# Hybrid decoder step on one core: unscaled token rows for the experts, the last cached values in front of weight slabs, stacked dilation-16 cache rows, and two state-space heads in two row strips

## The reference

```python
# state-space model: the decay between two positions, per head
rel = jnp.where(causal, cum[:, :, None] - cum[:, None, :], -jnp.inf)
w = cb[..., None] * jnp.exp(rel) * dtc[:, None]

# sample attention, group g: keys at distances 0, dil, ..., 128*dil (those that exist)
keys = jnp.concatenate([buf[:, :, 0], k], axis=1)
vals = jnp.concatenate([buf[:, :, 1], v], axis=1)
idx = wb + jnp.arange(S)[:, None] - dil * jnp.arange(129)[None, :]
p = softmax(q . keys[idx]);  o = p @ vals[idx]

# experts: the rows are normalised per token, h = x * rsqrt(mean(x*x) + eps) * gain
out = out + combine[..., e:e + 1] * swiglu(h, w_up[e], w_down[e])
```

## Time and profile before

| | |
|---|---|
| time of one execution, median of 3 (lowest, highest) | 2194.18 us (2193.89, 2195.5) |
| the profiled execution: its time, its span | 2194.97 us, 2193.2 us |
| mean granted TensorE clock of the profiled execution | 0.995 |
| layer 0 mixer and dense channel mixer | from 0 to some 840 us |
| layer 1 mixer and routing | to 1310.5 us |
| experts | 1310.5 to 2183 us |

### The profile page before, as it was taken

One profiled execution on the slowest core, in us unless ns is written; L12 is line 12 of the kernel. 1 busy time (PEld: TensorE's weight loads), 2 busy tenths in 40 slices (PEclk: granted clock), 3 DMA queues, 4 the chain that ended last, 5 costly groups with the idle time before them and its releaser, 6 DMA issues.

```text
span 2193.2 us, 43454 instructions
## 1 busy us (share of the span) xinstructions
PE 2155.8 (98%) x19497; PEld 1338.5 (61%) x19497; DVE 603.4 (28%) x1179; ACT 373.4 (17%) x671; POOL 103.9 (5%) x153
## 2 busy tenths in 40 slices
PE   7999999999999999999999989999999999999998
PEld 6777777767777777777777763534343434343435
DVE  5395323433110124933244331010101010101013
ACT  3323424311000023243333020000000000000000
POOL 2001020000000000011200010000000000000001
PEclk9999999999999999999999989999999999999999
DMA  5434535684444453354465759999999999999996
GB/s 160 135 101 138 165 109 158 174 242 135 135 137 114 132 168 123 116 160 126 131 176 141 245 228 378 410 405 415 406 415 406 414 407 415 402 412 404 407 415 247
DMA packets 298137, 548.66 MB, mean 250 GB/s; under 512 B 12153, under 2 KB 228603, under 8 KB 281504
## 3 DMA queue, kind: packets, MB, share of 16 engines
q1 hardware_dynamic: 289964, 535.84, 68.1%
q10 hardware_dynamic: 6644, 5.58, 0.8%
q0 software_dynamic: 1344, 4.45, 0.5%
HBM read 527.15 MB, written 22.50 MB: 251 GB/s over the span
## 4 chain that ended last, share of the span: by engine, by line
PE 95%; DVE 3%; issue 1%; ACT 1%; ACTq 0%; DMA 0%; DVEq 0%
PE bank L980 93%; PE bank L986 2%; ACT mem L1839 1%; DVE mem L2589 0%; DVE col L2592 0%; DVE mem L2560 0%; DVE mem L2281 0%; DVE mem L2602 0%; DVE mem L2605 0%; ACTq L2148 0%; DMA hv<-in_ssm_d_dram 0%; DVE mem L2285 0%; ACT L1839 0%; DVE mem L2600 0%; ACTq L2151 0%
## 5 line engine op out<-in xcount | busy, mean ns | idle before, releaser
L980 PE MATMUL bank<-mem 128*32 128x256 f32 (+11 forms) x11936 | 1007.3, 404 | 15.8 <-issue 5.3
L980 PEld LDWEIGHTS bank<-mem 128*32 128x32 f32 (+4 forms) x11936 | 567.8, 121 | 436.9 <-issue 236.0
L980 PE MATMUL bank<-hflat,mem 128*128 128x288 f32 (+1 forms) x2944 | 717.3, 407 | 1.3 <-ACT hflat L1839 0.7
L980 PEld LDWEIGHTS bank<-hflat,mem 128*128 128x128 f32 (+1 forms) x2944 | 538.0, 188 | 164.3 <-issue 20.3
L1839 ACT ACTIVATE mem<-bank 128x288 f32<-128x288 f32 (+7 forms) x344 | 157.2, 462 | 814.4 <-PE bank L980 775.4
L980 PE MATMUL bank<-mem,steps 128*32 128x384 f32 (+1 forms) x3072 | 289.8, 539 | 0.0
L980 PEld LDWEIGHTS bank<-mem,steps 128*32 128x32 f32 x3072 | 95.3, 110 | 191.1 <-issue 190.3
L2285 DVE SCALAR_TENSOR_TENSOR hflat<-hflat,bank 128x512 f32<-128x512 f32 x24 | 15.1, 682 | 411.1 <-ACT hflat L1839 411.1
L1839 ACT ACTIVATE hflat<-bank 128x512 f32<-128x512 f32 (+1 forms) x40 | 19.6, 554 | 566.0 <-PE bank L980 566.0
L2285 DVE SCALAR_TENSOR_TENSOR mem<-mem,bank 128x288 f32<-128x288 f32 (+1 forms) x93 | 43.2, 478 | 216.7 <-ACT mem L1839 178.6
L1839 ACT ACTIVATE mem<-mem 128x1152 f32<-128x1152 f32 (+8 forms) x102 | 80.2, 786 | 99.9 <-DVE mem L2359 71.4
(11 more groups left out here) (239 smaller groups left out, 720.3 us busy)
## 6 DMA issues: line engine op xcount, KB each, us to landing
mem<-in_w_moe_up_dram SPq DMA_DIRECT2D x64, 2048.0 KB, 18.1
mem<-in_w_moe_down_dram SPq DMA_DIRECT2D x56, 2048.0 KB, 18.9
mem<-in_w_moe_up_dram SPq DMA_DIRECT2D x32, 2304.0 KB, 20.1
mem<-in_w_in_dram SPq DMA_DIRECT2D x70, 1024.0 KB, 5.5
mem<-in_w_moe_up_dram SPq DMA_DIRECT2D x16, 1536.0 KB, 19.3
mem<-in_w_ffn_up_dram SPq DMA_DIRECT2D x44, 512.0 KB, 4.6
mem<-in_cache_kv_w_dram SPq DMA_DIRECT2D x26, 512.0 KB, 5.9
mem<-in_w_ffn_down_dram SPq DMA_DIRECT2D x16, 704.0 KB, 5.5
```

The source lines that it names most:

```text
L980: return mm(out, lhsT, rhs, start=start, stop=stop, skip_group_check=True)
```

## The change

Four edits, each with its bookkeeping.

1. **Token rows.** Both halves of `htok` are copied unscaled. The picking matrix of the first round holds each token's factor (`pick_scale`) in place of 1. After the gather, ScalarE multiplies `htok` by the factors in place, and only then may GpSimd scatter the rows. After a round VectorE sets `pick_scale` to 1.
2. **Last cached values.** The two slabs that stood in front of the wait for `att_o` and of the values of sequence 7 are issued behind them.
3. **Dilation-16 rows.** Two residues are stacked in 128 partitions: a 128 by 2 by 256 block (`kb_far`) by two DMAs. Keys: four transposes of 128 by 128 in place of eight of 64 by 128. Turned weights: two matmuls for four. Values: four matmuls of 128 rows by 128 columns for four of 64 rows by 256 columns. ScalarE's copy of the turned weights is 128 by 256 for 64 by 512.
4. **State-space heads.** ScalarE copies the running sums once more to partitions 32 to 39 (`cum_below`), and the odd head of a pair takes its row from there, so the two matmuls of a pair lie in different row strips of the array.

```diff
-        pT2 = view(arena, 9216 + 5 * P, 4, P)
+        pT2 = view(arena, 9216 + 5 * P, 2, P)
+        cum_below = steps[32:32 + SH, 2 * T:3 * T]
-        kb_half = [v[0:64, 5:9, :] for v in whole] + [view(steps[0:64, :], 0, 4, 256), view(over[0:64, :], 1280, 4, 256)]
+        kb_far = [v[:, 5:7, :] for v in whole] + [view(steps, 0, 2, 256), view(over, 1280, 2, 256)]
...
-                sp.dma_start(kb_half[i], c2048[:, 0:4, which, :]).then_inc(k_in[i], 16)
+                for e in range(2):
+                    sp.dma_start(kb_far[i][64 * e:64 * e + 64], c2048[:, e:4:2, which, :]).then_inc(k_in[i], 16)
...
                 for b in range(4, 7):
                     load_cache(L, 1, b)
-                weights_until(out0 + RING + 3)
                 sp.wait_ge(*filled(("att_o", L, 1)))
                 load_cache(L, 1, 7)
                 weights_until(out0 + RING + 4)
...
-            pool.wait_ge(token_rstd, 1)
-            pool.wait_ge(tok_half0, 3)
-            for b, (t0, n) in enumerate(BLK):
-                half = htokv[0:n, b, :, 0:P]
-                gp.tensor_tensor(half, half, t_rstd[0:n, b:b + 1].unsqueeze(2).to_broadcast([n, 4, P]), ALU.mult
-                                 ).then_inc(tok_scaled, 1)
-            pool.wait_ge(tok_scaled, 3)
-            pool.wait_ge(tok_half1, 3)
...
                 pool.wait_ge(slots_ready, r + 1)
+                pool.wait_ge(tok_scaled, 3 * r + 3)
...
-                close_bank(put(acc[:, 0:T], row_to(h, P), dts[0:SH, 2, :]), ("wdecay", L, h))
+                if h % 2 == 0:
+                    ins = put(acc[:, 0:T], row_to(h, P), dts[0:SH, 2, :])
+                else:
+                    row = ident[32:32 + SH, 32 + h:33 + h].to_broadcast([SH, P])
+                    ins = put(acc[:, 0:T], row, cum_below)
+                close_bank(ins, ("wdecay", L, h))
...
-                    for i in range(8):
-                        ins = turn(acc[:, 64 * i:64 * i + 64], half[:, i // 2, P * (i % 2):P * (i % 2) + P])
+                    for i in range(4):
+                        ins = turn(acc[:, P * i:P * i + P], far[:, i // 2, P * (i % 2):P * (i % 2) + P])
...
-                for r in range(4):
-                    c = 640 + 64 * r
-                    ins = turned(acc[0:64, P * r:P * r + P], kv_rows[:, c:c + 64])
+                for a in range(2):
+                    ins = turned(acc[:, P * a:P * a + P], kv_rows[:, 640 + P * a:768 + P * a])
...
                 for q in range(4):
-                    ins = put(acc[32 * q:32 * q + 32, c0:c0 + 256], pT2[0:64, q, cols], half[:, q, :],
+                    a, h0_ = q // 2, P * (q % 2)
+                    ins = put(acc[32 * q:32 * q + 32, c0 + h0_:c0 + h0_ + P], pT2[:, a, cols], far[:, a, h0_:h0_ + P],
                               False, b % 2 == 1)
...
-                pe.wait_ge(tok_scaled, 3)
+                pe.wait_ge(tok_half0, 3)
                 pe.wait_ge(tok_half1, 3)
...
                 act.wait_ge(*at("dt_cum", L))
+                step(fn(cum_below, dts[0:SH, 2, :], ACT.Copy))
...
-                copy_out(pT2[0:64].rearrange("p a r -> p (a r)"), key, psum(key)[0:64, :])
+                copy_out(pT2.rearrange("p a r -> p (a r)"), key, psum(key)[:, 0:2 * P])
...
-                    if half:
-                        ins = fn(out, src, ACT.Copy, scale=t_rstd[0:n, b:b + 1])
...
+                    ins = fn(out, src, ACT.Copy)
...
+            token_copies(1)
             act.wait_ge(token_rstd, 1)
-            token_copies(1)
...
+                for b, (t0, n) in enumerate(BLK):
+                    fn(htok[0:n, b, :], htok[0:n, b, :], ACT.Copy, scale=pick_scale[0:n, b:b + 1]).then_inc(tok_scaled, 1)
+                act.wait_ge(tok_scaled, 3 * r + 3)
+                act.sem_inc(wait_passed, 1)
                 act.wait_ge(x_scattered, 96 * (r + 1))
                 load_rows(1)
...
             dve.wait_ge(top_apart, 1)
+            step(ve.tensor_copy(pick_scale, t_rstd))
...
-                                     iota[0:n, 1:CAP + 1].rearrange("p (t f) -> p f t", f=TT), rank_0[0:n, b:b + 1], None,
-                                     ALU.is_equal).then_inc(picked, 1)
+                                     iota[0:n, 1:CAP + 1].rearrange("p (t f) -> p f t", f=TT), rank_0[0:n, b:b + 1],
+                                     pick_scale[0:n, b:b + 1], ALU.is_equal, ALU.mult).then_inc(picked, 1)
...
+                dve.wait_ge(tok_scaled, 3 * r + 3)
+                lstep(ve.memset(pick_scale, 1.0))
                 lstep(ve.tensor_scalar(rank2, rank2, float(-CAP), None, ALU.add))
```

More of the change, by code:

```diff
@@ L494, in cache_in @@
             i = order[n]
-            return k_in[i], 48 * (L * order.count(i) + order[:n + 1].count(i))
+            return k_in[i], 64 * (L * order.count(i) + order[:n + 1].count(i))
         def heads_of(g, first, n):
@@ L1395, in sample_keys @@
             def sample_keys(L, b, k):
-                rows, half = kb_rows[cache_buffer(0, b)], kb_half[cache_buffer(0, b)]
+                rows, far = kb_rows[cache_buffer(0, b)], kb_far[cache_buffer(0, b)]
                 acc = open_bank(("kT", L, b, k))
@@ L1429, in sample_scores @@
                         elif g == 2:
-                            keys = kt_[:, 1280:1792].rearrange("d (r p k) -> d r p k", r=4, p=2)[:, :, p, :]
-                            ins = put(near[rows, P:P + 256].rearrange("q (r k) -> q r k", r=4), q, keys,
+                            keys = kt_[:, 1280:1792].rearrange("d (a p k) -> d a p k", a=2, p=2)[:, :, p, :]
+                            ins = put(near[rows, P:P + 256].rearrange("q (a k) -> q a k", a=2), q, keys,
                                       pair == 0, False)
@@ L1481, in sample_values @@
                 acc = open_bank(key) if b % 2 == 0 else psum(key)
-                rows, half = kb_rows[cache_buffer(1, b)], kb_half[cache_buffer(1, b)]
+                rows, far = kb_rows[cache_buffer(1, b)], kb_far[cache_buffer(1, b)]
                 cols = slice(32 * pair, 32 * pair + 32)
@@ L2176, in token_copies @@
                     src = psum(key)[0:n, :].rearrange("t (k g f) -> t k g f", k=4, g=4)
[L2177 to L2184 removed]
+                    ins = fn(out, src, ACT.Copy)
+                    ins.then_inc((tok_half0, tok_half1)[half], 1)
+                    act.wait_ge((tok_half0, tok_half1)[half], b + 1)
                     act.sem_inc(bank_drained[jobs[key][0]], 1)
```

10 lines of the change are left out of this document (2 added, 8 removed).

## The result

The changed kernel took 2181.15 us (median of 6 runs, 2179.55 to 2183.96) where the kernel before, timed beside it, took 2194.84 (6 runs). The ratio is 0.9938, with a 95% interval of 0.9925 to 0.9950: 13.7 us or 0.6% faster. Predicted were 2179.0 us (2175.5 to 2184.0) and 15.2 us. The profiled execution took 2180.18 for 2194.97, with a span of 2178.4 for 2193.2: 14.8 us less.

A forecast was written before the change was run, and what follows sets the result against it. TensorE, busy for 98% of the span, was taken as the bound. Terms -3.9 - 2.3 - 1.1 - 6.9 - 1.2 + 0.2 = -15.2 us took the profiled 2194.97 to 2179.8, predicted as 2179.0 for the median; range 2175.5 to 2184.0.

The forecast's parts named there:

- head pairs: State-space heads (edit 4): a pair's two matmuls run side by side, 0.76 us for 1.25; eight pairs give -3.9 us.
- a sequence of values: Dilation-16 values (edit 3): 0.76 us for 1.24 without the 64-row form; -6.9 us in all.
- Both rivals on TensorE: Head pairs stay in series, 2182.9 us, chance 0.10; values bound by weight loads or issue, 2182.5, chance 0.12.
- The odd key steps: Key transposes (edit 3): faster transposes only lengthen TensorE's idle time behind them, 0.59 to 0.85 us; no gain.
- The even ones: Even key steps (edit 3): 0.29 us saved in each of eight over two layers, -2.3 us.
- So the order itself gives nothing: Edit 2, cached values of sequence 7: the new order gives and costs nothing; the old would wait 5.8 us in all.
- the paragraph on edit 2: Sequence 7's values: 2 MB at 250 to 355 GB/s take 6 to 8 us, landing some 3 us in hand.
- "Nothing" for what is moved: Edit 1's later scaling and scatters: rows 8.4 us later, 8 us of cover left at VectorE's turn; no cost.
- The gain ahead of the gather: Edit 1: VectorE's picks come sooner, so TensorE's 1.32 us idle time before the gather shrinks; -1.2 us.
- TensorE waits for no slab there, so a microsecond of its work is a microsecond of time.: Experts' stretch, 40% of the span: TensorE busy 872.4 of 872.45 us, so it was taken as the bound.
- the clock case: Rival at the gather: 6.8 us at half clock vanish with the idle gap, -18.6 us, 2175.6; chance 0.08.
- given back elsewhere: Rival: waits behind the values, for sequence 6 or 7 or first output slab, take say 13 us: 2192; chance 0.03.

The follow-up runs named there:

- experiment 10: Kernel before with edit 2 alone (cached values of sequence 7 ahead of two output slabs, still three DMAs a sequence): 2192.3 us for 2195.52, ratio 0.9981.
- experiment 2: Changed kernel with the two output slabs put back in front of the last cached values: 2188.9 us, ratio 0.9962 to the kernel before.
- experiment 3: Changed kernel with edit 1 undone (GpSimd scales half of the token rows ahead of the gather again): 2178.23 us, ratio 0.9908 to before.
- changed, slabs in halves: Changed kernel with every expert slab loaded by two DMAs, the first released after half of the replaced slab is used: 2177.92 us, ratio 0.9912 to before.
- edit 1 undone, late fetch: Changed kernel with edit 1 undone and the result rows fetched after slab 17 of the last expert for 16: 2177.8 us, ratio 0.9910 to before.
- edit 1 undone, halves, l. fetch: Changed kernel without edit 1, result rows fetched after slab 17, every expert slab asked for in two halves: 2178.08 us, ratio 0.9917 to before.
- experiment 6: Changed kernel, first two slabs of expert 4 loading half their bytes (2 MB fewer, products made with old data): 2175.91 us, ratio 0.9905 to before.
- experiment 7: Kernel before, first two slabs of expert 4 loading half their bytes (2 MB fewer): 2194.64 us for 2195.52, ratio 1.0001.
- Experiment 5: Changed kernel timed once more, no edit: 2181.03 us, ratio 0.9926 to the kernel before.
- experiment 11: Changed kernel with 32 small matmuls (128 TensorE instructions) in the idle time at the start: 2179.79 us, ratio 0.9927 to before.

## Why the prediction was right, and where it was not

**The passes.** The terms of edits 3 and 4 are as predicted: head pairs 0.76 (predicted 0.76), a sequence of values 0.76 (0.76), the steps of the table -3.1, -2.4 and -7.0 for -3.1, -2.3 and -7.1. Both rivals on TensorE fall: the pairs run side by side, and no load shows between the passes. The Trainium skill's page "TensorE: Matmul & The Clock Gate", section "LDWEIGHTS (loading the stationary operand)", has a load cost its columns over 1.2 GHz. The prediction took four such loads to stand in a row ahead of each pass, by which the two 64-column passes would have brought a sequence to an estimated 0.86. The trace does not agree with the row: the records of the four loads of a set start within 0.02 us of each other. What a single load costs is not tested by it. No run has edit 3 by itself; its share is the steps of this table.

**The odd key steps** were absorbed as predicted, with 0.78 us of idle time for a predicted 0.85. The even ones gave what was predicted: of the 3.1 us of the table's second row the four head pairs are 1.9, and the four even key steps the other 1.2.

**Edit 2: "So the order itself gives nothing".** This failed, on the good side. I read one execution, in which the values came 0.25 us in time, and took it for all. Alone the order gives 3 to 4 us (experiment 10), and together with edit 3 it avoids 5 to 8 us (experiment 2), for a predicted 5.8. The waits themselves were sized right, 2.90 and 2.77 for 2.9; the half clock behind them had no term. The 250 GB/s that the paragraph on edit 2 takes as the lower rate stands in none of the rows around that place (303 to 355); no term of the sum hangs on it.

**Edit 1: "Nothing" for what is moved.** This is the step that failed. The gain ahead of the gather was right in the profiled pair (-1.0 for -1.2), which were both at full clock there; in an execution at half clock there it is nothing (experiment 3). The scaling took 3.21 us on ScalarE for 3.3, and the scatters were issued later as worked out. I followed the moved rows to those who wait for them, VectorE's turn, and found 8 us of cover; 5.3 were left, so nobody waited. The difference is in the scatters' own landing: ScalarE's loads came 11.7 us behind the last scatter, for the 8.2 that I had taken over from before. I did not ask whose DMAs the scatters would meet. After, timelines of ScalarE, GpSimd and VectorE (the scaling, the first scatter and the last, the loads that wait for the scatters, VectorE's turn of the rows and its next work):

```profile
1291.93 3.21 ACT L1838 ACTIVATE mem<-mem 128x1024 f32<-128x1024 f32 x3
...
1296.08 1.23 POOL L926 DMA_INDIRECT xslots<-mem  x1 [84.21 <-ACT mem L1838]
...
1302.64 0.87 POOL L926 DMA_INDIRECT xslots<-mem  x1 [0.30 <-issue]
...
1315.16 2.62 ACTq L2212 DMA_DIRECT2D mem<-xslots  x4
...
1329.11 0.98 DVE L2962 STREAM_TRANSPOSE steps<-mem 128x768 f32<-128x768 f32 x1 [8.61 <-DMA mem<-xslots]
1335.42 1.88 DVE L2287 SCALAR_TENSOR_TENSOR hflat<-hflat,bank 128x512 f32<-128x512 f32 x3 [5.33 <-PE bank L974]
```

In experiment 3 the first scatter is issued 4.9 us ahead of the experts' start:

```profile
1291.46 1.22 POOL L926 DMA_INDIRECT xslots<-mem  x1 [3.66 <-DVE mem L2907]
```

In the changed kernel's profile it is 3.8 us behind the experts' start. Just behind that start lies a gap in the stream of slabs that cannot be filled: the seven slabs that fit are in, and the eighth waits until TensorE has used the first. Before, the scatters ran in and ahead of that gap. Now they run behind it, among slabs that follow each other without a pause. The GB/s of the changed kernel's DMAs from 1285 to 1312 us, in 40 slices, have the gap at 36 and 0 and the lower rate of the scatters behind it:

```profile
GB/s 401 388 485 425 388 400 461 425 437 401 388 449 400 437 413 255 73 36 0 382 394 316 376 267 218 316 388 388 309 431 376 394 419 358 404 419 440 443 413 391
```

The same view's row on the scatters, before (1303 to 1330 us) and after, has their median time from issue to landing:

```profile
xslots<-mem POOLq DMA_INDIRECT x6, 9.6
...
xslots<-mem POOLq DMA_INDIRECT x6, 11.0
```

The slab landings of the traces, set against TensorE's fixed pace of 108.4 us an expert, show what that costs. Slabs are counted through all eight experts, 21 in each, from 0. Us from the last part's landing to the slab's use (worked out, good to about half a microsecond; below zero TensorE waits):

```
kernel                          slab 9   slab 84   slab 165   slab 166   slab 167 (last)
before                           18.6      12.0       6.2        3.8        0.6
edit 1 alone                     16.7       9.5       3.2       -1.0       -1.5
changed                          16.2       8.7       1.6       -3.1       -2.8
changed, once more               16.5       9.1       2.6       -1.5       -2.4
changed, slabs in halves         17.9       9.4       3.8       -1.3       -2.4
edit 1 undone                    19.4      12.7       6.7        4.3        1.4
changed, 2 MB fewer              15.8      10.0       6.5        3.8        1.3
before, 2 MB fewer               17.6      13.9      11.6       11.7        9.6
heads alone                      18.6      10.4       3.1       -0.1       -1.4
order alone                      18.9      10.7       3.9        1.1       -0.7
edit 1 undone, late fetch        17.5      11.2       3.7        4.7        0.0
edit 1 undone, halves, l. fetch  18.1      11.7       5.2        5.9        3.0
changed, old slab order          15.5       7.7      -0.6       -2.9       -3.5
changed, shifted                 15.9       8.8       1.6       -2.8       -2.9
```

Among the kernels with whole slabs and all their bytes, those with edit 1 have 15.5 to 16.7 us of cover at slab 9 and 7.7 to 9.5 at slab 84, those without it 17.5 to 19.4 and 10.4 to 12.7: no two of them overlap, so edit 1 takes about 2 to 3 us of cover in the first expert. It never comes back, since the slabs lose another 12 to 16 us against TensorE by slab 165 in every kernel that loads all its bytes, the one before too. There the last slab was 0.6 us in time. So the loss that began at 1296 us shows 860 us later. That the scatters' place is what takes the cover is read from the timelines; no run moved the scatters alone. The table also shows how little the kernel before had to spare: with the heads or the order alone, without edit 1, TensorE waited 1.1 and 0.3 us for the last slab.

**"TensorE waits for no slab there, so a microsecond of its work is a microsecond of time."** The first half was true, the second does not follow. The same row has the DMAs at a share of 1.00 and 401 GB/s beside TensorE's 872.38 of 872.45: two resources without a gap, and either can be the bound. The Trainium skill, "Perfetto Trace Analysis", section "Roofline", puts what the 16 DMA engines of a core can move at about 435 GB/s; this trace agrees over long stretches: 401 GB/s over the experts before, 400 after. Single slices of 0.7 us have up to 485. The page "DMA: Bandwidth & Descriptors", section "Issuing engines are not separate DMA queues", says that transfers of all issuing engines interleave on the same DMA engines, and this trace agrees: where the scatters of GpSimd run among the slabs of SyncE they take 11.0 us to land for 9.6.

**How the sum came out right.** The changed kernel has ratios of 0.9938, 0.9926 and, shifted, 0.9927; without edit 1 it has 0.9908, 0.9910 and, with halves, 0.9917. So edit 1 costs the changed kernel some 4 us (2 to 6.6 by the single pairs) where -1.2 was predicted; alone it costs 2 (from -0.9 to +4.6). The intervals of single pairs touch, so the size is loose; the sign rests on the three pairs together and on the table of landings. That the stream of slabs sets the changed kernel's end rests on experiment 6 beside experiment 7. Edit 2 gives 3 to 4 where 0 was predicted. The two misses, some 5 us and 3 to 4 the other way, nearly cancel. A prediction of 15.2 against 13.7 is therefore right in the passes and lucky in the rest.

**The clock.** I gave the clock case a chance of 0.08 and one event. The profile had three shorter stretches at half clock and one new one. Experiment 5 shows that this changes between executions of one kernel by 3.4 us of time at half clock in several places; it is of the size of the spread of the timed runs (2177.3 to 2184.0), and no part of the median can be put down to it.

**The rival "given back elsewhere"** had 0.03 and named the cached values and the output slabs. Giving back did happen, 4.3 us in the profile, at a place that it did not name.

Left open: why the last of a slab's 16 parts falls farther behind its first (2 us in the first expert, 10 in the fifth, 11 to 13 from the sixth on, 17 at slab 166). While the last two slabs land, the changed kernel's DMAs run at half their rate (GB/s from 2135 to 2165 us in 40 slices), as if a part of the DMA engines were done and the others behind. What these carry more was not tried.

```profile
GB/s 415 399 404 415 426 426 410 410 431 415 399 410 399 415 404 410 404 399 191 224 224 202 180 202 218 186 197 202 208 202 229 131 60 0 0 0 0 0 0 0
```

## What to carry to other kernels

When a step is moved, follow its DMAs as well as its result: a transfer that ran in a gap cost nothing here, and the same transfer among others that set the pace cost 2 to 3 us of their cover, which was missed a long way behind. Where a stage table has two resources at 1.00, ask for the cover of the last transfer, not whether one waited. A transfer that lands within half a microsecond of its use in one profile was late in others; an order that puts it in front was worth time by itself. An idle time that is shorter after a change is no gain as long as the clock just ahead of it differs. And undo each edit of a faster change alone: here one of four made it slower.

## What the runs showed of the hardware

- **Stops that move with the program.** TensorE's stops with no releaser among the values of layer 0 and in the gather, 0.6 to 1.5 us, begin 1 to 2 us behind the start of a 16 KB transfer on the queue that loads instructions (one between 467.0 and 467.6 us, ahead of the stop that ends at 469.54). With 128 instructions more at the start the one at 469 us was gone and one stood at 1294, in the gather (experiment 11). That TensorE then waits for its instructions is what this fits; it was not measured by itself. The values at 0.76 us a sequence issue 48 instructions in that time; that this density is why the stop shows there now was not tested. Other stops of this kind, 0.67 near 142 and 890 us and 1.46 behind the last fold of layer 1, kept their place in every kernel and begin 2 to 15 us behind such a transfer; they are not explained.
- **Two matmuls of 8 rows by 128 columns in different row strips ran side by side** like those of 64 rows: 0.76 us for the pair, against 1.23 behind each other in the same view.
- **Four weight loads of 32 columns into four column strips started within 0.02 us of each other,** and 24 of them with their 24 matmuls took 0.76 us.
- **Half clock, mostly behind short gaps, and differently each time.** The two executions of the changed kernel had the lower level for 17.1 and 23.9 us ahead of the end, in stretches of 3.4 and 6.8 us. Most begin behind waits and stops of 0.8 to 2.4 us; the one at 1283 us of the second begins where TensorE had not been idle for 16 us, among transposes and small matmuls. Behind the waits of 2.9 and 2.8 us of experiment 2 it was over 13 us each. In the stage table of the second execution (experiment 5), one stretch of each length (us, busy, clock, DMA):

```profile
1266.40:1273.00 6.60, 6.37 (x15) 0.50 0.00 0
1283.50:1286.70 3.20, 3.20 (x18) 0.52 0.92 379
```
